# Output stage of a hybrid decoder step: the products of the two column halves alternate between two PSUM banks

## The reference

```python
def merge_out(x, o_attn, az, o_gla, gz, mg_a, mg_b, gla_norm_w, w_attn_out, w_gla_out, w_out):
    o_gla = rms_norm(o_gla, gla_norm_w)...
    ya = jnp.einsum('bsc,cd->bsd', o_attn.astype(x.dtype) * jax.nn.silu(az), w_attn_out)
    yb = jnp.einsum('bsc,cd->bsd', o_gla * jax.nn.silu(gz), w_gla_out)
    mixed = jax.nn.sigmoid(mg_a) * ya + jax.nn.sigmoid(mg_b) * yb
    return x + jnp.einsum('bsd,de->bse', mixed, w_out)
```

## Time and profile before

| | |
|---|---|
| three executions | 2471.91, 2473.31, 2473.87 us |
| median | 2473.31 us |
| profiled execution: span, from its first instruction to its last | 2470.5 us |
| PE busy, share of the span | 2439.6 us, 99% |
| DVE, ACT busy | 1205.1 us, 906.3 us |
| output stage, first branch product to last matmul | from 2063.3 to 2461.7 us |

### The profile page before, as it was taken

One profiled execution on the slowest core, in us unless ns is written; L12 is line 12 of the kernel. 1 busy time (PEld: TensorE's weight loads), 2 busy tenths in 40 slices (PEclk: granted clock), 3 DMA queues, 4 the chain that ended last, 5 costly groups with the idle time before them and its releaser, 6 DMA issues.

```text
span 2470.5 us, 37105 instructions
## 1 busy us (share of the span) xinstructions
PE 2439.6 (99%) x13710; PEld 1956.6 (79%) x13710; DVE 1205.1 (49%) x2860; ACT 906.3 (37%) x2163; POOL 199.2 (8%) x367
## 2 busy tenths in 40 slices
PE   9999999999999999999999999999999998999998
PEld 6888887887778888887787888788778755888887
DVE  5323432334321115565665666556756447655663
ACT  5224534443332214223544545545334233212221
POOL 0000000000000000112111111222222100000000
PEclk9999999999999999999999999999999999999999
DMA  6333323332332223457677666787677799444341
GB/s 193 103 121 115 104 92 127 104 101 92 111 107 98 91 89 122 142 170 243 210 221 227 199 210 209 220 287 226 210 227 218 221 346 349 165 153 165 141 155 69
DMA packets 209122, 416.99 MB, mean 169 GB/s; under 512 B 32512, under 2 KB 53520, under 8 KB 206832
## 3 DMA queue, kind: packets, MB, share of 16 engines
q1 hardware_dynamic: 166912, 293.60, 35.6%
q0 software_dynamic: 29712, 95.06, 13.3%
q10 hardware_dynamic: 12320, 25.96, 2.8%
HBM read 313.33 MB, written 112.99 MB: 173 GB/s over the span
## 4 chain that ended last, share of the span: by engine, by line
PE 94%; DMA 2%; DVE 2%; ACT 1%; issue 0%; SPq 0%; POOL 0%; DVEq 0%; ACTq 0%
PE b_acc L1231 20%; PE b_acc L1233 19%; PE b_acc L1232 19%; PE c_p_s L1281 3%; PE c_p_o L1304 3%; PE c_p_qk L1268 3%; PE c_p_t L1292 3%; PE f_p_b L2002 2%; PE f_p_b L2004 2%; PE f_p_b L2003 2%; PE f_p_z L2002 2%; PE f_p_z L2004 2%; PE f_p_z L2003 2%; PE b_acc L1237 1%; PE b_acc L1238 1%; PE e_p_o L1923 1%
## 5 line engine op out<-in xcount | busy, mean ns | idle before, releaser
L1231 PE MATMUL b_acc<-b_whi,hT_hi 128*128 128x512 f32 x2048 | 817.9, 399 | 4.0 <-DVE b_wlo L967 1.9
L1233 PE MATMUL b_acc<-b_whi,hT_lo 128*128 128x512 f32 x2048 | 799.3, 390 | 0.0
L1232 PE MATMUL b_acc<-b_wlo,hT_hi 128*128 128x512 f32 x2048 | 797.9, 390 | 0.0
L1231 PEld LDWEIGHTS b_acc<-b_whi,hT_hi 128*128 128x128 f32 x2048 | 384.6, 188 | 90.9 <-issue 8.7
L1233 PEld LDWEIGHTS b_acc<-b_whi,hT_lo 128*128 128x128 f32 x2048 | 384.5, 188 | 82.7
L1232 PEld LDWEIGHTS b_acc<-b_wlo,hT_hi 128*128 128x128 f32 x2048 | 385.3, 188 | 74.2
L967 DVE SCALAR_TENSOR_TENSOR b_wlo<-b_raw,a_lnw,b_whi 128x512 fp32r<-128x512 f32 x268 | 192.7, 748 | 364.6 <-ACT b_whi L759 364.2
L773 ACT COPY b_stage<-b_acc 128x512 f32<-128x512 f32 (+2 forms) x198 | 115.3, 582 | 506.6 <-PE b_acc L1233 496.1
L797 ACT ACTIVATE c_sm<-c_sm,c_ends 128x256 f32<-128x256 f32 (+1 forms) x384 | 172.9, 452 | 81.6 <-DVE c_ends L1052 81.6
L759 ACT ACTIVATE b_whi<-b_raw,a_lnw 128x512 fp32r<-128x512 f32 x268 | 182.9, 714 | 4.1 <-ACT c_og L815 1.9
L771 ACT ACTIVATE b_stage<-b_acc 128x512 f32<-128x512 f32 x96 | 57.4, 598 | 306.4 <-PE b_acc L1233 306.2
(11 more groups left out here) (320 smaller groups left out, 3153.4 us busy)
## 6 DMA issues: line engine op xcount, KB each, us to landing
b_raw<-in_w_in SPq DMA_DIRECT2D x134, 512.0 KB, 4.2
tm<-b_stage SPq DMA_DIRECT2D x256, 256.0 KB, 2.1
a_x<-tm POOLq DMA_DIRECT2D x192, 256.0 KB, 4.8
b_ck<-in_cache_kv_w POOLq DMA_DIRECT2D x104, 256.0 KB, 5.0
c_qk<-tm SPq DMA_DIRECT2D x101, 256.0 KB, 3.6
f_m<-tm SPq DMA_DIRECT2D x16, 1024.0 KB, 5.8
c_v<-tm SPq DMA_DIRECT2D x53, 256.0 KB, 4.2
og<-c_og ACTq DMA_DIRECT2D x48, 264.0 KB, 3.8
```

Of the source, the lines that this page charges most:

```text
L1231: nc.tensor.matmul(out, stat_hi, mov_hi, start=(k == 0), stop=False)
L1232: nc.tensor.matmul(out, stat_hi, mov_lo, start=False, stop=False)
L1233: return nc.tensor.matmul(out, stat_lo, mov_hi, start=False, stop=(k == KC - 1))
```

## The change

`product` takes a list of outputs, one for each half, and issues each of its three kinds of matmul for both halves before the next kind: hi by hi into bank 0 and bank 1, hi by lo into both, lo by hi into both. The loop over the depths `c` is now the outer one, and both halves are summed at a time, each in its bank. The same matmuls are done, with the same operands; only their order differs. `out_products(t)` does both halves in one go, and so can't be split around a transpose any more: `transpose_branches(2)` now follows both halves of tile 0, and `transpose_mixed(16)` both halves of tile 15. The last tile keeps its two halves apart. Each tile signals `g2_done` once, after both halves, as before (the last tile once for each half).

```diff
--- before.py
+++ after.py
@@ -1995,13 +1995,16 @@
                                                gates[t % 2][0:r, (G4 * a + c) * P:(G4 * a + c + 1) * P], ident[0:r, 0:r])
             last.then_inc(bT_step, 1)
 
-        def product(t, out, stat_hi, stat_lo, mov_hi, mov_lo, first, last):
-            if t == SAMPLE_AT:
-                nc.tensor.matmul(out, stat_hi, mov_hi, start=first, stop=False)
-                return nc.tensor.matmul(out, stat_hi, mov_lo, start=False, stop=last)
-            nc.tensor.matmul(out, stat_hi, mov_hi, start=first, stop=False)
-            nc.tensor.matmul(out, stat_hi, mov_lo, start=False, stop=False)
-            return nc.tensor.matmul(out, stat_lo, mov_hi, start=False, stop=last)
+        def product(t, outs, stat_hi, stat_lo, mov_hi, mov_lo, first, last):
+
+            for e, out in enumerate(outs):
+                nc.tensor.matmul(out, stat_hi, mov_hi[:, e * CH:(e + 1) * CH], start=first, stop=False)
+            for e, out in enumerate(outs):
+                done = nc.tensor.matmul(out, stat_hi, mov_lo[:, e * CH:(e + 1) * CH], start=False, stop=last and t == SAMPLE_AT)
+            if t != SAMPLE_AT:
+                for e, out in enumerate(outs):
+                    done = nc.tensor.matmul(out, stat_lo, mov_hi[:, e * CH:(e + 1) * CH], start=False, stop=last)
+            return done
 
         def branch_products(t, parts=(0, 1)):
             if t == 1 and parts == (0,):
@@ -2019,10 +2022,10 @@
                     pe.wait_ge(w_lo, 2 * G4)
                     pe.wait_ge(outed, 2 * NPAIR - 1)
                     pe.wait_ge(g_u_read, DB * NP)
-                for e in range(0, D, CH):
-                    for c in range(G4):
-                        last = product(t, p_b[:, a, e:e + CH], bT_hi[:, a, c, :], bT_lo[:, a, c, :],
-                                       wb_hi[:, a, c, e:e + CH], wb_lo[:, a, c, e:e + CH], c == 0, c == G4 - 1)
+                outs = [p_b[:, a, e:e + CH] for e in range(0, D, CH)]
+                for c in range(G4):
+                    last = product(t, outs, bT_hi[:, a, c, :], bT_lo[:, a, c, :], wb_hi[:, a, c, :], wb_lo[:, a, c, :],
+                                   c == 0, c == G4 - 1)
             if a == 1:
                 last.then_inc(g1_done, 1)
             elif t == 0:
@@ -2038,7 +2041,7 @@
                                            m[0:r, t % 2, 0, c * P:(c + 1) * P], ident[0:r, 0:r])
             last.then_inc(mT_step, 1)
 
-        def out_products(t, e):
+        def out_products(t, halves=(0, CH)):
             out, hi, lo = (p_b[:, 0, :], lT_hi, lT_lo) if t == LAST else (p_z, mT_hi, mT_lo)
             pe.wait_ge(mT_step, 3 * t + 3)
             if t == LAST:
@@ -2048,11 +2051,11 @@
             else:
                 pe.wait_ge(w_lo, 2 * G4 + KC)
                 pe.wait_ge(g_o_evacd, 1)
+            e, stop = halves[0], halves[-1] + CH
+            outs = [out[:, a:a + CH] for a in halves]
             for c in range(KC):
-                last = product(t, out[:, e:e + CH], hi[:, c, :], lo[:, c, :],
-                               wo_hi[:, c, e:e + CH], wo_lo[:, c, e:e + CH], c == 0, c == KC - 1)
-            if e or t == LAST:
-                last.then_inc(g2_done, 1)
+                last = product(t, outs, hi[:, c, :], lo[:, c, :], wo_hi[:, c, e:stop], wo_lo[:, c, e:stop], c == 0, c == KC - 1)
+            last.then_inc(g2_done, 1)
 
         def tail(q):
             if q == 1:
@@ -2106,21 +2109,17 @@
             branch_products(1, (0,))
             transpose_mixed(0)
             branch_products(1, (1,))
-            out_products(0, 0)
+            out_products(0)
             transpose_branches(2)
-            out_products(0, CH)
             transpose_mixed(1)
             for t in range(2, TILES):
                 branch_products(t)
                 if t + 1 < TILES:
                     transpose_branches(t + 1)
-                out_products(t - 1, 0)
-                if t < LAST:
-                    out_products(t - 1, CH)
+                out_products(t - 1)
                 transpose_mixed(t)
-            out_products(LAST - 1, CH)
-            out_products(LAST, 0)
-            out_products(LAST, CH)
+            out_products(LAST, (0,))
+            out_products(LAST, (CH,))
 
         return tail, main
```

## The result

The changed kernel takes 2479.17 us (median of 9 runs, 2477.87 to 2481.07), the kernel before 2472.28 us on the same chip (9 runs, 2471.46 to 2474.95). The ratio is 1.0024, with a 95% interval of 1.0015 to 1.0033: slower. The two medians lie 6.9 us apart, where 4.6 us was forecast; the interval of the ratio is 3.7 to 8.2 us, so the times alone do not tell 6.9 from 4.6, and it is the profiles that do. The profiled execution took 2478.47 us, and its span is 2476.7 us, 6.2 us more than the 2470.5 us before. What lies around the span is 1.8 us in it.

The account below looks back on a forecast made before the run. The prediction took the kernel to be bound by its sequence of PE instructions. Its terms, 0 + 1.86 + 2.77 = +4.63 us on 2473.31 us, gave 2477.9 us, with a range of 2475 to 2481 us.

Parts of the forecast that it names:

- rival 3: PE's clock falls at the two new waits; one fall gives 2479.5 us, two give 2481.1 us; chance 0.08.
- Part 1, the alternation: Output stage: 1552 matmuls change order between banks, at an unchanged 226.6 ns each; 0 us.
- the one switch of banks: Old order's change of bank in the out products: distances of 0.22 and 0.23 us, as the same-bank average of 226.6 ns.
- Rivals 1 and 2: Output stage: alternating pays, up to 20.6 us, chance 0.08; or alternating costs, 2485.7 us at 5 ns each, chance 0.06.
- Part 2, the start: Tiles 0 to 2: transposes of the mix of tile 1 wait uncovered for DVE's split, PE late by 1.86 us.
- the relay: Start of the stage: transposes at 2102.91, ACT's split 2103.98, DVE's split 2105.03, PE's transposes of the mix 2106.39.
- rival 4: The start's wait is taken back by a later load or split, only the end counts: 2476.1 us, chance 0.03.
- Part 3, the end: Tiles 15 and 16: out products of tile 16 wait for the split, 2.59 us late, 2.77 us with slower first matmuls.
- The restart: Out products of tile 16: first 24 matmuls behind a wait take 5.62 us against 5.44, 0.18 us more.
- What lies around the span: Outside the profiled span: the median of the runs was put 2.8 us above it.

Follow-up runs that it names:

- experiment 2: The kernel before, not alternating, with only the second half of tile 15 moved ahead of the transposes of the mix of tile 16; 2476.19 us, ratio 1.0018.
- 3: The kernel before, not alternating, with only the transposes of tile 2's branches moved behind both halves of tile 0; 2476.62 us, ratio 1.0017.
- 4: The changed kernel with 9 extra matmuls, results unused, in the wait ahead of the out products of tile 16; 2477.68 us, ratio 1.0020.
- 6: The kernel before with 20 extra matmuls ahead of the branch products of tile 0 and 5 ahead of those of tile 1; 2472.44 us, ratio 1.0000.
- experiment 5: The changed kernel with 9 extra matmuls, results unused, in each of its two new waits; 2477.45 us, ratio 1.0020.
- the first experiment: The changed kernel, still alternating, with out products of tiles 0 and 15 split by depth, 24 matmuls before and 24 behind the transposes; 2473.55 us, ratio 1.0004.
- 9: The changed kernel, still alternating, with out products of tiles 0 and 15 cut into 36 matmuls before and 12 behind the transposes; 2473.86 us, one run.

## Why the prediction was right, and where it was short

The terms that the sum has came out as forecast, and the measured time, 2479.17 us, lies in the range of 2475 to 2481 us. It lies 0.2 us outside the 2477 to 2479 us that the forecast gave itself without its rivals, and what is in it beyond the terms is the clock of rival 3. That the time is only 1.3 us off is in part luck: the change was forecast 2.3 us too small, but on a base, the median of three executions, that was 1.0 us too high (2473.31 against 2472.28 us of nine).

- *Part 1, the alternation, 0 us.* Right: 226.75 ns a matmul, tiles of 23.56 us, and by itself a ratio of 1.0004 (0.9996 to 1.0013). From tile 1 to tile 16 the two orders differ by 0.02 us in 339.8. The step that carried it was the distance at the one switch of banks in the old order: that single place foretold 1552 matmuls. It was read more sharply than it allows, for the difference of two rows with two decimals is open by 10 ns and not by 5. Rivals 1 and 2 are out.
- *Part 2, the start, +1.86 us.* Measured 1.91, with 0.07 us from ahead of the place, so 1.84. Each station of the relay came within 0.05 us of the forecast: transposes 2102.95 (2102.91), ACT 2104.02 (2103.98), DVE 2105.07 (2105.03), PE 2106.44 (2106.39). Nothing took the delay back: the tiles behind keep their length, and rival 4 is out. What the term lacks is that its base moves with a load: it is 1.84 us beside the profile that it was read from and 2.40 us beside that of experiment 2 (see 3).
- *Part 3, the end, +2.59 and +0.18 us.* Measured 2.50 for the wait. All of the 0.09 us between is the last leg: DVE to PE was borrowed from the start, at 1.36 us, and is 1.28 us here. The restart shows in the kernel with the end filled (4), whose clock held: 10.79 us from the first to the last of the 48 matmuls' starts, where 47 distances of 226.6 ns are 10.65, so 0.14 us.
- *The step that fell short: the clock.* The forecast had no term for it and left it to rival 3, at 0.08; both profiles of the changed kernel have it. Behind bare waits of 2.4 us the clock fell in 3 of 5 cases at the start and in 3 of 4 at the end, and behind both of nearly 3 us ahead of the second branch products of tile 0 (6); behind the three filled ones, and behind covered or shorter ones at these places, never. Its size was right, 1.6 us each time, by the counting of matmuls in the earlier trace rows; its chance was not. The error was in reading *one* window that kept its 1.00 with PE busy for 0.26 us as the behaviour of such waits. It was one case, and the same wait in the same program has since been seen both ways. So have the waits ahead of the stage: one of 2.98 us in the kernel before kept its 1.00, one of 2.81 us at the same instruction in experiment 5 did not.
- *What lies around the span* was taken as 2.8 us, the median less the profiled span; it is 1.8 us (2478.47 − 2476.7, and 1.7 to 1.9 in every other profiled run of the experiments). The other 1 us was the scatter between executions of the kernel before. With it the forecast's own sum is 2475.1 + 1.8 = 2476.9 us; the kernel with both waits filled took 2477.45, the changed one 2479.17, and the 1.7 us between them are about one fall. (The chances of rival 3 were also added up loosely: one fall gives 6.2 us by its own figures, beyond 0.2%, yet only 0.06 of its 0.08 was counted as slower.)

What stays open: what decides, in one execution, whether a fall comes. Nine bare waits of this length, one or two profiles of a kernel, are too few for a rate; and if one in three such waits keeps its clock anyway, three filled ones could all have kept it by chance once in 27 times. That falls account for the whole 1.7 us between the unfilled and the filled kernel is an inference from the size of one and the medians; their intervals overlap. The mean granted clock, on record for every execution to 0.001, points the same way: it averages 0.9969 over the 17 executions of the changed kernel, 0.9974 over the 11 with both waits filled and 0.9976 over 57 of the kernel before. One fall, 3.4 us at half clock in 2477 us, is 0.0007.

## What to carry to other kernels

Two orders of the same matmuls, same bank or other bank, cost the same here; look for a switch in the old order before expecting anything of it. What counts in such a reordering is which work stood behind a transpose or another hand-over as its cover: read the relay's length from the timeline (3.4 us here, of which the transposes themselves take 1.0) and keep at least the rest queued behind the transposes: 12 matmuls of 0.23 us did here, and 24 were not needed. If a wait of some microseconds on the bounding engine can't be covered, allow for one fall of the clock in its price (1.6 us here), or fill it with work that nobody reads: behind three filled waits no fall was seen, and the wait stayed.

## What was not expected of the hardware

- A fixed 13.3 ns stand in each matmul at full clock beside its columns, with 512 and 256 moving columns alike. A shorter weight load (134 ns instead of 188) does not make them smaller; with it they were 16.7 ns.
- The same wait of 2.45 us in the same program is followed by clock 1.00 in one execution and 0.50 in another. This is not all of the scatter between runs: it is 1.9 us with both waits filled (11 runs) and 3.2 and 6.2 us with both bare (9 and 8 runs), but also 6.0 us in the kernel of the first experiment, which has neither (11 runs).
- Half clock in the first branch products cost nothing, and one wait further on it cost 1.5 us (6): the granted clock is a loss only where PE is what the rest waits for. A PE that kept its clock in the first stretch waited longer behind it, and the clock fell there instead, in two of the twelve profiles (experiments 1 and 9).
